# Gated scan on one core: near scores in three pieces, keys and update in other banks, a new order of every queue, and the merges' turn between the halves

## What is computed

```python
def chunked_gated_scan(q, k, v, log_g):
    # S_t = diag(exp(log_g_t)) S_{t-1} + k_t^T v_t ; o_t = q_t S_t
    ...
def bidir_scan(q, k_f, k_b, v, lg_f, lg_b):   # forward, and backward over flipped time
    ...
for layer in range(2):
    h = rms_norm(x, norm_pre[layer])
    proj = h @ w_in[layer]
    ...
    # 4 heads of 32 key channels; gate log_sigmoid(a @ wa2 + ba) / 16, a of rank 16
    y_a = gla_branch(gq, gk, gv, gg, gaf, gab, ...)
    y_b = diff_branch(dq, dk, dv, dg, ...)        # softmax attention, not touched
    # 4 heads of 64 channels; f = lb + (1 - lb) sigmoid(z), key (1 - lb) sigmoid(-z)
    y_c = hgrn_branch(hq, hzf, hzb, hi, hg, ...)
    # a branch ends: o = rms_norm(o per head, norm_w); merge_heads(o) * silu(g)
    y = jnp.concatenate([y_a, y_b, y_c], -1) @ w_out[layer]
    x = x + rms_norm(y, norm_post[layer])
```

## Time and profile before

| | us |
|---|---|
| three runs | 3787.21, 3793.72, 3800.80 |
| median | 3793.72 |
| the profiled execution | 3787.14 |
| its span | 3785.2 |
| PE busy, x36396 matmuls | 3158.4 (83%) |
| PE's weight loads, x36396 | 2683.3 (71%) |
| DVE busy | 2023.9 (53%) |
| ACT busy | 1309.7 (35%) |
| POOL busy | 331.2 (9%) |
| first scan | 569 to 850 |
| first merge | 878 to 1024 |
| second scan | 1576 to 1840 |
| second merge | 1886 to 2034 |

### The profile page before, as it was taken

How to read it: one execution, slowest core, us unless ns; L and a number is a source line. 1 busy time by engine, 2 the same in 40 slices (tenths; PEclk the granted TensorE clock), 3 DMA queues, 4 the chain that set the end, 5 groups by cost and what they waited for, 6 DMA issues and landing times. The chain is left out here.

```text
span 3785.2 us, 83074 instructions
## 1 busy us (share of the span) xinstructions
PE 3158.4 (83%) x36396; PEld 2683.3 (71%) x36396; DVE 2023.9 (53%) x3501; ACT 1309.7 (35%) x2342; POOL 331.2 (9%) x242
## 2 busy tenths in 40 slices
PE   7999996765899999756478998789898788886699
PEld 7988884554698888645357997777777577775344
DVE  3455445667625555476585266456665444553452
ACT  3133324543422333355253122234444122221541
POOL 0200000001002000020010021011110122221100
PEclk9999996767999999866689999899999699898899
DMA  3532213214436221231352444553331321112330
GB/s 126 172 102 79 79 38 109 75 31 161 159 101 193 81 77 49 62 93 31 109 173 101 152 157 140 181 172 97 109 117 43 104 48 45 41 40 76 139 108 33
DMA packets 268260, 378.76 MB, mean 100 GB/s; under 512 B 45173, under 2 KB 207277, under 8 KB 266552
## 3 DMA queue, kind: packets, MB, share of 16 engines
q1 hardware_dynamic: 165834, 260.49, 22.2%
q10 hardware_dynamic: 102066, 112.97, 8.6%
HBM read 256.42 MB, written 118.94 MB: 99 GB/s over the span
## 5 line engine op out<-in xcount | busy, mean ns | idle before, releaser
L385 PE MATMUL psum<-proj_w_low,h_high 128*128 128x344 f32 (+1 forms) x1984 | 667.6, 336 | 18.2 <-DVE proj_y L411 15.1
L385 PE MATMUL psum<-proj_w_high,h_high 128*128 128x344 f32 (+1 forms) x1984 | 656.8, 331 | 0.0
L385 PE MATMUL psum<-proj_w_high,h_low 128*128 128x344 f32 (+1 forms) x1984 | 655.9, 331 | 0.0
L385 PEld LDWEIGHTS psum<-proj_w_low,h_high 128*128 128x128 f32 x1984 | 375.8, 189 | 33.7 <-DVE proj_y L411 16.7
L385 PEld LDWEIGHTS psum<-proj_w_high,h_high 128*128 128x128 f32 x1984 | 375.8, 189 | 6.8
L385 PEld LDWEIGHTS psum<-proj_w_high,h_low 128*128 128x128 f32 x1984 | 375.4, 189 | 7.1
L385 PE MATMUL psum<-proj_rest_w_low,h_high 128*128 128x304 f32 x640 | 209.0, 327 | 33.4 <-DVE proj_rest_w_low L400 21.9
L411 DVE COPY proj_y<-psum 128x344 f32<-128x344 f32 (+1 forms) x130 | 70.4, 542 | 243.7 <-PE psum L385 235.3
L385 PE MATMUL psum<-proj_rest_w_high,h_low 128*128 128x304 f32 x640 | 196.0, 306 | 0.0
L385 PE MATMUL psum<-proj_rest_w_high,h_high 128*128 128x304 f32 x640 | 196.0, 306 | 0.0
L1161 DVE COPY diff_wt<-psum 128x512 f32<-128x512 f32 x64 | 44.3, 692 | 282.5 <-PE psum L1107 282.5
(11 more groups left out here) (405 smaller groups left out, 6698.0 us busy)
## 6 DMA issues: line engine op xcount, KB each, us to landing
proj_raw<-in_w_in SPq DMA_DIRECT2D x24, 1376.0 KB, 6.9
proj<-proj_y ACTq DMA_DIRECT2D x192, 172.0 KB, 1.8
delta_x<-dn_qkv SPq DMA_DIRECT2D x40, 384.0 KB, 5.2
proj<-proj_y ACTq DMA_DIRECT2D x68, 224.0 KB, 2.0
dn_prep_x<-proj SPq DMA_DIRECT2D x54, 256.0 KB, 3.6
proj_raw<-in_w_in SPq DMA_DIRECT2D x7, 1792.0 KB, 8.1
modulate_w<-in_mod_w SPq DMA_DIRECT2D x16, 768.0 KB, 5.0
merge_z<-proj SPq DMA_DIRECT2D x8, 1536.0 KB, 8.1
```

The lines of the kernel that those rows point to most:

```text
L385: last = PE.matmul(self.ps[:, j % self.banks, 0:self.width], hp[:, kt, tokens], wp[:, c % 2, kt, :], start=kt == 0 and n == 0, stop=kt == ...
```

## The change

In the scan:

- The 32-row scores are issued in three pieces: levels 0 to 2, levels 3 to 5, and the last two levels. Level 6, two crossed quarters in 16 matmuls of 32 rows, becomes 8 of 64 rows. 120 matmuls a tile become 112; each float32 matmul stands in the trace as two, so 240 become 224.
- The turned keys and the update go to banks 4 and 5, those of the 64-row scores. The keys wait for `made64` of the same tile, the next tile's first 64-row scores for `fed` (u), and the 32-row scores for the last outputs' copy only.
- The keys `kts` have two buffers, by n % 2. SP's load of tile n waits for `updated(n - 3)`. The 32-row masked copies come before the last 64-row ones.
- Due times are new on every engine; `PACKS` and `GROWTHS` give one for each level in place of `at_level`. DVE makes the keys ahead of the decay, and ACT copies q and k ahead of its exponential for `decay_a`. The modulation's pieces and their addition have other due times too.

In the merge PE turns tile n + 1 between the two halves of tile n, DVE's copy of tile n + 1 goes behind the residual add, ACT's copy behind the logs, and the start is written out anew.

```diff
-    PERIOD = 22
-    LEAD, LEVEL = 17, 1.22
+    PERIOD, LEAD = 22, 21
+    PACKS, GROWTHS = (0.7, 0.8, 1, 2.3, 3.6, 3.9, 5.9), (-1.8, 0.3, 1.6, 2.9, 3.7, 3.9, 11.1)
...
+        self.at, self.lt, self.kts, self.qts = t("at", [16, 2, P]), t("lt", [P, 2, P]), t("kts", [P, 2, 2, 3, P]), t("qts", [P, 2, 3, P])
...
-                SP.wait_ge(*self.attended(n - 3))
+                SP.wait_ge(*self.updated(n - 3))
...
-        yield -17
+        yield -20.3
...
-        yield -12.9
+        yield -17.6
...
-        yield -11.8
+        yield -17
...
-        yield 8.8
+        yield 7.1
         PE.wait_ge(*self.keys_grown(LEVELS * n + LEVELS - 1))
-        if n:
-            PE.wait_ge(*self.o_copied(n - 1))
+        PE.wait_ge(*self.made64(n))
...
-                last = PE.transpose(ps[:, r, j * P:j * P + P], self.kts[:, r, j, :], ident[:])
+                last = PE.transpose(ps[:, 4 + r, j * P:j * P + P], self.kts[:, n % 2, r, j, :], ident[:])
         last.then_inc(*self.keys.inc())
-        yield 11
+        yield 16.4
...
-                last = PE.matmul(ps[:, r, at:at + w], self.kn[:, r, j * P:(j + 1) * P], nat[:, col:col + w], start=True, stop=True)
+                last = PE.matmul(ps[:, 4 + r, at:at + w], self.kn[:, r, j * P:(j + 1) * P], nat[:, col:col + w], start=True, stop=True)
...
             return last
-        yield self.at_level(4) + 0.4
+        def near32(levels):
+            for l in levels:
+                for a in range(4):
+                    for h in range(4):
+                        score32(l, h, 32 * a, 32 * a, 32, 32 * l)
+        yield -2.1
         PE.wait_ge(*self.diagonal(n))
+        PE.wait_ge(*self.keys_packed(LEVELS * n + 1))
+        PE.wait_ge(*self.queries_packed(LEVELS * n + 1))
+        if n:
+            PE.wait_ge(*self.o_copied(n - 1))
+        near32(range(3))
+        yield 1
         PE.wait_ge(*self.keys_packed(LEVELS * n + 2))
         PE.wait_ge(*self.queries_packed(LEVELS * n + 2))
         if n:
-            PE.wait_ge(*self.made64(n - 1))
+            PE.wait_ge(*self.fed(n - 1))
         for l in range(4):
             last = scores64(l, l, False)
         last.then_inc(*self.scored.inc())
-        yield 11.3
-        PE.wait_ge(*self.placed(3 * n))
+        yield 3.6
+        PE.wait_ge(*self.keys_packed(LEVELS * n + 4))
+        PE.wait_ge(*self.queries_packed(LEVELS * n + 4))
+        near32(range(3, 6))
+        yield 4.9
         PE.wait_ge(*self.keys_packed(LEVELS * n + LEVELS - 1))
         PE.wait_ge(*self.queries_packed(LEVELS * n + LEVELS - 1))
+        for l in (6, 7):
+            for key in (0, 64):
+                for h in range(4):
+                    query = key if l == 6 else 64 - key
+                    last = score32(l, h, key, query, 64, 192 + query)
+        last.then_inc(*self.scored.inc())
+        yield 5.2
+        PE.wait_ge(*self.placed(3 * n))
         for l in range(4, 8):
             last = scores64(l, l - 4, l == 7)
         last.then_inc(*self.scored.inc())
-        yield 14.5
-        PE.wait_ge(*self.keys_packed(LEVELS * n + LEVELS - 1))
-        PE.wait_ge(*self.queries_packed(LEVELS * n + LEVELS - 1))
-        PE.wait_ge(*self.fed(n))
-        for l in range(6):
-            for a in range(4):
...
+        yield 14.9
...
+        yield -8.5
+        V.wait_ge(*self.sig_k(n))
+        if n >= 2:
+            V.wait_ge(*self.keys(n - 2))
+        for j in range(2):
+            keyed = V.tensor_scalar(kt[:, :, 1 + j, :], self.by_channels(sg[:, 1], j), self.oml[:, j:j + 1], None, ALU.mult)
+        keyed.then_inc(*self.keyed.inc())
+        yield -6.9
...
-        V.wait_ge(*self.sig_k(n))
-        if n:
-            V.wait_ge(*self.keys(n - 1))
-        for j in range(2):
-            keyed = V.tensor_scalar(kt[:, :, 1 + j, :], self.by_channels(sg[:, 1], j), self.oml[:, j:j + 1], None, ALU.mult)
-        keyed.then_inc(*self.keyed.inc())
...
-            yield self.at_level(l) + 0.6
+            yield self.GROWTHS[l - 1]
...
-        yield 13
+        yield 24.7
         V.wait_ge(*self.updated(n))
-        V.tensor_tensor(self.u[:, n, 0], ps[:, 0, :], self.heads[:], ALU.mult)
-        V.tensor_tensor(self.u[:, n, 1], ps[:, 1, :], self.heads[:], ALU.mult).then_inc(*self.fed.inc())
+        V.tensor_tensor(self.u[:, n, 0], ps[:, 4, :], self.heads[:], ALU.mult)
+        V.tensor_tensor(self.u[:, n, 1], ps[:, 5, :], self.heads[:], ALU.mult).then_inc(*self.fed.inc())
...
-        yield 17.6
+        yield 7.1
         V.wait_ge(*self.scored(3 * n + 1))
+        for l in range(self.GLA_LEVELS):
+            placed = place32(l)
+            if l < self.GLA_LEVELS - 1:
+                vo.chain(placed)
+        placed.then_inc(*self.placed.inc())
+        yield 9.5
...
-        yield 20
-        V.wait_ge(*self.scored(3 * n + 2))
-        for l in range(self.GLA_LEVELS):
-            placed = place32(l)
-            if l < self.GLA_LEVELS - 1:
-                vo.chain(placed)
-        placed.then_inc(*self.placed.inc())
...
-        for n in (1, 2):
-            self.dve_sums(n)
-            self.dve_gate(n)
+        self.dve_sums(1)
+        self.dve_gate(1)
+        self.dve_sums(2)
+        self.dve_copy(1)
+        self.dve_gate(2)
...
-            if n + 1 < NT:
-                self.dve_copy(n + 1)
...
+            if n and n + 1 < NT:
+                self.dve_copy(n + 1)
...
+        self.act_logs(1)
+        self.act_sigmoid(1)
+        self.act_logs(2)
+        self.act_copy(1)
+        self.act_sigmoid(2)
...
-            if n + 1 < NT:
-                self.act_copy(n + 1)
...
+            if n and n + 1 < NT:
+                self.act_copy(n + 1)
...
-            if n and n + 1 < NT:
-                turn(n + 1)
...
+                if n and half and n + 1 < NT:
+                    turn(n + 1)
...
-        return self.scan.PERIOD * (j // 2) + self.scan.LEAD + (-8.8, -2)[j % 2]
+        return self.scan.PERIOD * (j // 2) + self.scan.LEAD + (-16.5, -0.2)[j % 2]
...
-            yield self.when(j) + 1.7
+            yield self.when(j) + (17.8, 3.3)[j % 2]
```

89 lines of the change are left out of this document (37 added, 52 removed).

## The result

| | before | after | forecast |
|---|---|---|---|
| median, us | 3790.9 (4 runs, 3787.21 to 3800.80) | 3661.64 (4 runs, 3652.49 to 3670.57) | 3668 (3630 to 3715) |
| profiled execution, us | 3787.14 | 3652.49 | 3662 |
| its span, us | 3785.2 | 3650.2 | |
| ratio | | 0.965, interval 0.9621 to 0.9679 | 0.967 |

A forecast was written before the change was run, and what follows sets the result against it. No engine was full; each scan tile was a chain of waits, and two waits held the merges. Gains of 59 (first scan), 41 (second) and 25 us (merges), 125 off 3787.1, gave 3662, or 3668 as a median; range 3630 to 3715.

The forecast's parts named there:

- What bounds, and what the order does: Scans: scoring and growing alternate, DVE waiting at L712 for all 240 score matmuls; the new order would overlap them.
- Period of the first scan, 24.4: First scan: a step-by-step walk of one tile through the engines gave 24.4 us for 31.5.
- the outputs at 3.5 and the update at 3.3 us: First scan, PE: times per tile taken from earlier rows of 2.87 to 3.68 and 2.84 to 3.6 us.
- rival (a): Scans: less idling grants PE more clock, periods near 22 and 21.5 us, total 3642; chance 0.14.
- my 42.6: First scan: gain from six periods, each 7.1 us shorter; part of that scan's sum of 59 us.
- Second scan, 41 us: Second scan: tile 3's late load holds the start, then five periods of 23.4 us; ends at 1799.5 for 1840.5.
- Rival (b): Scans: one "issue" stall of 2.5 us a tile stays on the path, 30 us back, total 3698; chance 0.21.
- A switch of matmul shape costs nothing: PE in the scans: about five more tiling switches a tile, read as free from the trace, so nothing in the sum.
- Merges, 25 us: Both merges: turning the next tile between matmul halves, 12.1 us a tile, gains 12.2 and 14.5 us, 25 together.
- The term that failed is the work of the next stage: Merges: L400, 3 us on DVE, was said to eat a little of the 12.2 and 14.5 us, leaving 25.
- Slower (c): Scans: every packet boundary between scores stalls, 13.7 us on each of 12 periods, total 3833; chance 0.03.
- no change (d): Scans: waits for u or late loads hold each tile 10 us, scoring and growing still alternate, total 3789; chance 0.04.

The follow-up runs named there:

- one_block: The changed kernel with all 32-row scores in one block at the third piece's place: 25.3 us a tile in the first scan, 25.0 in the second.
- kts_single: The changed kernel with one buffer of keys in place of two: 24.2 us a tile in the first scan, 23.2 in the second.
- banks_back: The changed kernel with turned keys and update back in banks 0 and 1: 27.2 us a tile in the first scan, 26.9 in the second.
- pe_minus: The changed kernel without the second piece of 32-row scores (levels 3 to 5): 20.6 us a tile in the first scan, 21.6 in the second.
- split_late: The changed kernel with the next stage's first split (L400, DVE) moved behind the merge's copy of tile 7: profiled span 3648.8 us for 3650.2.
- unchanged kernels: Kernels whose first scan is that of the changed kernel: mean 21.9 us a tile in the first scan, 22.5 in the second.

## Why the prediction held, and where it did not

- **What bounds, and what the order does.** Right. L712 waited for the whole block of scores, and the new order lets scoring and growing overlap. `one_block`, `kts_single` and `banks_back` show that each part is needed and that the loss of none brings the old 31.5 back. L712 was less than half of it: of the 66 us that DVE stood idle in six tiles, 24.7 were there and 27.0 behind the update and the modulation.
- **Period of the first scan, 24.4.** Measured 21.35, and 21.9 as the mean of six kernels. The steps that failed are the outputs at 3.5 and the update at 3.3 us: the rows show 1.90 and 1.97, together 2.9 less. I took them at the clock of before, though the change itself takes the idle stretches away in which that clock fell. In the second scan, where the clock stayed low at 0.67, outputs took 3.51 us and the update 3.2 to 3.8, near the 3.68 and 3.2 costed. Shorter terms at a higher clock are what rival (a) said, at 0.14; its 22 is the measured period of the first scan, its 21.5 for the second was not reached. The shorter period alone gave 61.0 us in six tiles for my 42.6. The ends of this scan came as worked out: 9.5 for 10.4 ahead of tile 1, 6.9 for 6.1 behind the last.
- **Second scan, 41 us.** 40.8. The load of tile 3 held it, with 16.5 us of waiting for the 17 expected, and its turns came 76.3 us after the first ones for 78.3 before, 2.0 of gain for the 2.5 expected. From its turns on, the period was 22.45 for 23.4, and most of what that gave, the additions on GpSimd took: tile 3's own L715 came 18.0 us after its turns, where the next tile took 11.8.
- **Issue stalls.** The forecast had none on the path. Between 8.8 and 11.5 us of them stayed in six tiles, and DVE waited for part of that. Rival (b) had the mechanism, as the packets show, but about twice the size or more: `pe_minus`, with no such stall in the first scan and 1.0 us less work, is 1.3 us a tile faster, not 2.5. In the sum this was hidden under the terms that were too long.
- **A switch of matmul shape costs nothing.** Wrong, though small. The reading compares a start with the end of the matmul before, and the profile models those ends. The starts of single matmuls say more. In the changed kernel's first scan, 32-row matmuls start 0.01 us apart, and the first L572 or L1562 starts 0.12 after the last of them. L567 start 0.11 apart, and the first L603 comes 0.20 after the last; L1562 0.16 apart, and the first L612 0.26 after. So a switch costs about 0.1 us. A tile has ten for seven before; by these figures that is an estimated 0.3 us a tile, some 4 us in all, which the sum put at nothing.
- **Merges, 25 us.** 15.3. The turn between the halves runs as worked out (12.0 us a tile in `split_late`, for 12.1), and the start gave 3.8 of 4.2. The term that failed is the work of the next stage, costed at under 2 us: it stands ahead of DVE's copy on the ring's own engine and cost 5 in each merge, as `split_late` shows.
- **Slower (c) and no change (d).** Neither came. (c) decides from 2.7 stalls a tile. One block of 112 matmuls has one of 3.2 us a tile in the mean, beside one of 0.23; the unchanged kernels have about one, of 1.6.

So the total was right partly because two misses of 18 and 10 us lie on opposite sides. That is luck.

Open: which packets cost a stall, since they fall at fixed places of the program and most of them cost none; by what way GpSimd's additions hold one-input instructions; how much the granted clock by itself adds to a period; and what the new due times, the form of level 6 and SP's new condition give, as none of them was changed alone.

## To carry to other kernels

When a change removes idle stretches, take PE's terms at the clock it will then be granted, at least as one end of the range. Cut long runs of very short matmuls with other work in between, even at no gain in overlap: in them PE can use up instructions faster than these arrive. And look at every queue that shares the stretch, SP's and GpSimd's too, before counting a gain: here one wait for a load and one series of additions decided what two engines' better order was worth.

## What the runs showed of the hardware

- GpSimd's additions in SBUF (2.2 to 2.5 us each) stretch DVE's SBUF instructions to about their own length, 0.56 to 2.57 us and 0.95 to 2.96, and leave those that read PSUM alone.
- The granted clock of the first scan was 0.93 in the changed kernel and 0.88 to 0.92 in five others with the same first scan, 0.85 with one block, 0.79 with three waits more on PE, 0.73 before. All have 2590 to 2690 trace matmuls in six tiles.
- An instruction packet is 256 instructions (12 packets more or fewer for 3072 instructions). PE's stalls named "issue" end 1.2 to 1.6 us after a packet has landed, in all 85 over 0.3 us in six tiles of thirteen first scans. They were up to 4.1 us in a block of 224 trace matmuls, and absent in a first scan where 128 of them a tile stood in two pieces.
- Between matmuls of different tile shapes lay 0.12 to 0.26 us from start to start, about 0.1 more than within one shape.
- In code that no kernel changed, 1758 us long, a mean clock of 0.92 in place of 0.94 is 21 us.
